# A hybrid layer pair: new order and new PSUM banks in the prepare stage of the recurrent branch

## The reference, cut to what matters

```python
us = token_shift(u_shift, mu[0], mu[1])             # r, k, v, w_in, a_in
w_log = -softplus(-(w0 + einsum('blde,def->dblf', tanh(w_in), w2))) - 0.5
decay = exp(-exp(w_log))                            # low-rank product 1, two directions d
a = sigmoid(a0 + einsum('blde,def->dblf', a_in, a2))   # low-rank product 2, the "rate"
kkf = to_heads(k * k_k)
kk = kkf * rsqrt(maximum(sum(kkf * kkf, -1), 1e-24))   # the norms
k_dir = to_heads(k)[None] * (1 + (a - 1) * to_heads(k_a)); b_dir = kk[None] * a
y = y_f + y_b                                       # of the two scans
yn = (y - mean) * rsqrt(var + LNX_EPS) * lnx_g + lnx_b
bonus = sum(r * (k_dir[0] + k_dir[1]) * r_k, -1) * v
out = (yn + bonus) * silu(gate)
```

## Time and profile before

| | |
|---|---|
| median of three runs | 3101.37 us |
| span of the profiled execution (first to last instruction) | 3091.2 us, 10.2 us below that median; the page gives no other time of that execution |
| busy: PE, DVE, ACT, POOL | 2874.3, 1512.4, 964.4, 771.8 us |
| the four prepare stages | 40.10, 44.70, 45.85 and 40.05 us, 170.70 us together |

### The profile page before, as it was taken

How to read it: one execution, slowest core, us unless ns; L and a number is a source line. 1 busy time by engine, 2 the same in 40 slices (tenths; PEclk the granted TensorE clock), 3 DMA queues, 4 the chain that set the end, 5 groups by cost and what they waited for, 6 DMA issues and landing times. The chain is left out here.

```text
span 3091.2 us, 61066 instructions
## 1 busy us (share of the span) xinstructions
PE 2874.3 (93%) x25648; PEld 2134.9 (69%) x25648; DVE 1512.4 (49%) x2768; ACT 964.4 (31%) x2248; POOL 771.8 (25%) x977
## 2 busy tenths in 40 slices
PE   6989998999998998999999989998999798999999
PEld 4968787886563786764588856645888576458674
DVE  5654636454433854541464246427833774265552
ACT  2021213122432124551221137511212574112561
POOL 3312223130013430011222214225531432244000
PEclk8999999999999999999999989999999899999999
DMA  6230100001332112121211152020111311212100
GB/s 225 81 113 19 39 4 16 17 32 59 110 103 101 55 55 96 56 83 41 83 52 47 66 188 77 11 95 34 55 55 55 124 55 56 87 47 89 58 1 28
DMA packets 108049, 206.16 MB, mean 67 GB/s; under 512 B 21795, under 2 KB 25394, under 8 KB 107264
## 3 DMA queue, kind: packets, MB, share of 16 engines
q1 hardware_dynamic: 107504, 201.36, 18.6%
q0 software_dynamic: 272, 0.89, 0.1%
HBM read 186.91 MB, written 15.54 MB: 65 GB/s over the span
## 5 line engine op out<-in xcount | busy, mean ns | idle before, releaser
L665 PE MATMUL psum<-weights,h_t 128*128 128x256 f32 x1488 | 352.0, 379 | 0.8 <-ACT p_u_u L749 0.8
L665 PEld LDWEIGHTS psum<-weights,h_t 128*128 128x128 f32 x1488 | 279.6, 190 | 38.5 <-ACT p_u_u L749 1.2
L1299 DVE TENSOR_REDUCE neg_max<-psum 128x1 f32<-128x768 f32 (+1 forms) x192 | 159.8, 864 | 220.4 <-PE psum L1169 174.8
L665 PE MATMUL psum<-z_l,x_tiles 128*128 128x256 f32 x816 | 192.8, 379 | 0.0
L665 PEld LDWEIGHTS psum<-z_l,x_tiles 128*128 128x128 f32 x816 | 155.0, 190 | 21.1
L1862 PE MATMUL psum<-weights,q_l 128*128 128x512 f32 x384 | 166.5, 592 | 0.0
L760 ACT ACTIVATE square<-psum 128x512 f32<-128x512 f32 (+1 forms) x80 | 45.0, 565 | 378.5 <-DVE psum L1017 242.0
L1190 PE MATMUL psum<-eye,prob 128*128 128x128 f32 x832 | 135.9, 286 | 11.3 <-DVE prob_t L1317 3.9
L1346 POOL TENSOR_TENSOR z_l<-z_l,inv_total 128x128 f32<-128x128 f32 x80 | 31.9, 399 | 428.7 <-DVE inv_total L1310 428.7
L1264 ACT ACTIVATE prob<-psum,neg_max 128x768 f32<-128x768 f32 (+1 forms) x160 | 129.7, 816 | 18.6 <-DVE neg_max L1299 12.4
L1862 PEld LDWEIGHTS psum<-weights,q_l 128*128 128x128 f32 x384 | 72.2, 190 | 87.1 <-issue 87.1
(11 more groups left out here) (445 smaller groups left out, 6175.9 us busy)
## 6 DMA issues: line engine op xcount, KB each, us to landing
weights<-in_ada_w_dram SPq DMA_DIRECT2D x30, 2048.0 KB, 8.0
weights<-in_a_w_in_dram SPq DMA_DIRECT2D x10, 2048.0 KB, 8.7
weights<-in_b_w_in_dram SPq DMA_DIRECT2D x8, 2048.0 KB, 9.2
weights<-in_c_w_in_dram SPq DMA_DIRECT2D x8, 2048.0 KB, 9.1
weights<-in_w_in_dram SPq DMA_DIRECT2D x6, 2048.0 KB, 7.7
x_aside<-x_tiles SPq DMA_DIRECT2D x24, 512.0 KB, 2.6
x_tiles<-x_aside SPq DMA_DIRECT2D x4, 3072.0 KB, 12.8
weights<-in_a_w_out_dram SPq DMA_DIRECT2D x4, 2048.0 KB, 8.0
```

What stands on the lines that cost most here:

```text
L665: last = pe.matmul(dst, lhs[:, k, :], rhs[k // 2][:, k % 2, :], start=k == 0, stop=k == KH - 1)
L1299: last = dve.tensor_reduce(neg_max[:, i % 4, m:m + 1], score(i, m, 0, keys), AX, ALU.max, negate=True)
```

## The change

All in the prepare stage; no instruction's operands change but for the banks:

- **PE.** The low-rank product of the decay comes first, before the norm sums, with both 256-column context parts (they now share bank 5); the 512-column part of the rate follows the norm sums. For p > 0 three eighths of the first projection stand before the spreading of the norms, the rest behind it. The low-rank products of d = 1 follow. y is turned before the last projection, v and the bonus rows after it. Pair 0 has one half of the modulation sums before the spreading, the other behind.
- **DVE.** The decay scan of d = 0 starts before kk is made; the last three operations on y come after direction 0, and y's gate after direction 1. DVE, in place of ACT, copies v and the bonus out of PSUM, at the end of the stage.
- **ACT** takes the first latent tile before the second `decays`, the second before the second `exponentials` (p > 0), and moves tile x - 1 between the square and the scaling of tile x.
- **POOL** raises the norms to their power before y's. The second `decays` waits for k_f only, not for r_f.

```diff
     def lat_bank(x):
-        return pr.bank(0 if x % 2 else 2)
+        return pr.bank(1 if x % 2 else 7)
 
     def turn_bank(x):
-        return pr.bank(3 if x % 2 else 1)
+        return pr.bank(3 if x % 2 else 2)
...
+                    move(x - 1)
                 if x >= 2:
                     act.wait_ge(*turned.at(x - 1))
...
                     act.activation(gate_rows[:, c, :], pr.bank(c), ACT.Copy).then_inc(*mod_copied.tick())
-            act.wait_ge(*v_turned.at(1))
-            if p:
-                act.wait_ge(*y_ready.at(1))
-            act.activation(b["v_tok"][:, 0:XC, :], pr.bank(1).rearrange("p (c i) -> p c i", i=HEAD), ACT.Copy)
-            act.activation(b["v_tok"][:, XC:NC, :], pr.bank(3)[:, 0:CTX].rearrange("p (c i) -> p c i", i=HEAD),
-                           ACT.Copy).then_inc(*bonus_out.tick())
-            early = 1 if units[0][0] == "kv" else 0
-            if early:
+            else:
                 take(0)
             decays(1)
-            if not early:
-                take(0)
+            take(1 if p else 0)
             exponentials(1)
-            for x in range(1, len(units)):
+            for x in range(2 if p else 1, len(units)):
...
             pool.wait_ge(*pool_chained.at(1))
+            pool.wait_ge(*norms.at(2))
...
-                    pe.matmul(pr.bank(5 + 2 * j)[:, 0:CTX], lora[s, j, P * p:P * p + P], src[s, GAP:US],
-                              start=True, stop=True).then_inc(*lora_done.tick())
+                src = (w_in, a_in)[j]
+                return pe.matmul(lora_ps(j)[ctx], lora[s, j, P * p:P * p + P], src[s, GAP:US] if ctx else src[s, 0:SEQ],
+                                 start=True, stop=True)
+
+            def lora_decay(d):
+
+                if d:
+                    pe.wait_ge(*exp_done.at(2))
+                lora_part(d, 0, 0)
+                lora_part(d, 0, 1)
+                lora_part(d, 1, 1).then_inc(*lora_done.tick())
+
+            def lora_rate(d):
+                lora_part(d, 1, 0).then_inc(*lora_done.tick())
...
                     pe.wait_ge(*moved.at(x - 1))
                 else:
-                    pe.wait_ge(*bonus_out.at(1))
+                    pe.wait_ge(*kk_done.at(1))
...
-                    w = pr.weights.get(pe, first_chunk + chunk_at[kind])
-                if x >= 2:
-                    pe.wait_ge(*read_out(x - 2))
-                elif x == 0:
-                    pe.wait_ge(*kk_done.at(1))
-                elif p:
-                    pe.wait_ge(*y_gated.at(1))
-                else:
-                    pe.wait_ge(*mod_copied.at(1))
...
+                    if x >= 2:
+                        pe.wait_ge(*read_out(x - 2))
+                    elif x and p == 0:
+                        pe.wait_ge(*mod_copied.at(2))
+                for f in range(a, e):
...
+            def turn_v():
+                pe.wait_ge(*exp_done.at(4))
...
+            def bonus_rows():
+                pe.wait_ge(*prods.at(1))
...
+            lora_decay(0)
+            norm_sums()
+            lora_rate(0)
             if p == 0:
-                pe.wait_ge(*mod_copied.at(2))
-            for c in range(NC):
-                for h in range(2):
-                    s = slice(64 * h, 64 * h + 64)
-                    last = pe.matmul(pr.bank(1 if c < XC else 3)[s, CH * (c % XC):CH * (c % XC) + CH],
-                                     v[s, col_of(c):col_of(c) + CH], pr.eye[s, s], start=True, stop=True)
-            last.then_inc(*v_turned.tick())
-            for x in range(len(units)):
+                mod_sums_of(0)
+                spread_norms()
+                mod_sums_of(1)
+            else:
+                project(0, 0, 3)
+                spread_norms()
+                project(0, 3, KT)
+            lora_decay(1)
+            lora_rate(1)
+            for x in range(1 if p else 0, len(units)):
                 project(x)
                 if x and x - 1 in lat:
                     turn(x - 1)
+                if p and x == len(units) - 2:
+                    turn_y()
             if p == 0:
-                pe.wait_ge(*exp_done.at(4))
                 for c in range(2):
                     mod_columns(pe, gate_sums[:, 8 * c:8 * c + 8], gate_rows[:, c, :], pick).then_inc(*mod_turned.tick())
...
+            turn_v()
+            bonus_rows()
             if len(units) - 1 in lat:
                 turn(len(units) - 1)
...
             y, bonus, square = b["y"][:, 0, :, :], b["bonus"][:, :, :], b["y_square"].rearrange("p (c i) -> p c i", c=XC)
+            for gap in (kk, dec, rate):
+                dve.memset(gap[:, SEQ:GAP], 0.0)
...
             if p:
+                link(dve.reduce_sum(stat[:, 1, :], square, AX))
+                dve.tensor_scalar(stat[:, 1, :], stat[:, 1, :], 1.0 / HEAD, LNX_EPS, ALU.mult, ALU.add)\
+                    .then_inc(*y_squared.tick())
                 link(dve.tensor_tensor(bonus, bonus, b["v_tok"][:, 0:XC, :], ALU.mult))
                 link(dve.tensor_tensor(bonus, bonus, wide(lnx[:, 1, previous, :], 1, XC), ALU.add))
-                dve.wait_ge(*y_rooted.at(1))
-                link(dve.tensor_tensor(y, y, wide(stat[:, 3, :], 2, HEAD), ALU.mult))
-                link(dve.tensor_tensor(y, y, wide(lnx[:, 0, previous, :], 1, XC), ALU.mult))
-                dve.tensor_tensor(y, y, bonus, ALU.add).then_inc(*y_ready.tick())
-            dve.wait_ge(*spread.at(1))
-            for gap in (kk, dec, rate):
-                dve.memset(gap[:, SEQ:GAP], 0.0)
-            dve.scalar_tensor_tensor(kk[:, 0:SEQ], k[:, 0:SEQ], kk_w, pr.bank(2), ALU.mult, ALU.mult)
-            dve.scalar_tensor_tensor(kk[:, GAP:US], k[:, GAP:US], kk_w, pr.bank(3)[:, 0:CTX], ALU.mult, ALU.mult)\
-                .then_inc(*kk_done.tick())
-            dve.wait_ge(*kk_done.at(1))
...
                 link(dve.tensor_tensor_scan(run[:, flip], resets[:, d, flip], dec[:, flip], 0.0,
                                             ALU.mult, ALU.add))
                 dve.tensor_tensor(ex[:, :], run[:, :], dec[:, :], ALU.subtract).then_inc(*summed.tick())
+                if d == 0:
+                    dve.wait_ge(*spread.at(1))
+                    dve.scalar_tensor_tensor(kk[:, 0:SEQ], k[:, 0:SEQ], kk_w, pr.bank(2), ALU.mult, ALU.mult)
+                    dve.scalar_tensor_tensor(kk[:, GAP:US], k[:, GAP:US], kk_w, pr.bank(3)[:, 0:CTX], ALU.mult, ALU.mult)\
+                        .then_inc(*kk_done.tick())
+                    dve.wait_ge(*kk_done.at(1))
                 dve.wait_ge(*exp_done.at(2 * d + 2))
...
                 dve.tensor_tensor(b["b_f"][:, d, :], rate[:, :], dec[:, :], ALU.mult)
-                link(dve.tensor_tensor(b["k_f"][:, d, :], kd[:, :], dec[:, :], ALU.mult))
+                dve.tensor_tensor(b["k_f"][:, d, :], kd[:, :], dec[:, :], ALU.mult).then_inc(*used.tick())
+                dve.wait_ge(*used.at(d + 1))
                 dve.wait_ge(*exps.at(d + 1))
-                dve.tensor_tensor(b["r_f"][:, d, :], b["r_f"][:, d, :], r, ALU.mult).then_inc(*used.tick())
+                dve.tensor_tensor(b["r_f"][:, d, :], b["r_f"][:, d, :], r, ALU.mult)
                 if d == 0 and p:
-                    dve.wait_ge(*y_turned.at(1))
-                    dve.tensor_tensor(mix_t[:, previous, :], pr.bank(0), gate_s[:, previous, :], ALU.mult)\
-                        .then_inc(*y_gated.tick())
+                    dve.wait_ge(*y_rooted.at(1))
+                    link(dve.tensor_tensor(y, y, wide(stat[:, 3, :], 2, HEAD), ALU.mult))
+                    link(dve.tensor_tensor(y, y, wide(lnx[:, 0, previous, :], 1, XC), ALU.mult))
+                    dve.tensor_tensor(y, y, bonus, ALU.add).then_inc(*y_ready.tick())
             dve.scalar_tensor_tensor(ksum[:, :], ksum[:, :], rk_w, r, ALU.mult, ALU.mult).then_inc(*prods.tick())
-            if p == 0:
+            if p:
+                dve.wait_ge(*y_turned.at(1))
+                dve.tensor_tensor(mix_t[:, previous, :], y_ps, gate_s[:, previous, :], ALU.mult)
+                dve.wait_ge(*y_ready.at(1))
+            else:
                 g = PCOL["ada_b"] + 16
                 dve.wait_ge(*mod_turned.at(2))
                 dve.tensor_tensor(pr.modulation[:, 16:24, :], gate_sums.rearrange("p (f v) -> p f v", v=2),
                                   wide(pr.par[:, g:g + 8], 2, 2), ALU.add)
+            dve.wait_ge(*v_turned.at(1))
+            dve.tensor_copy(b["v_tok"][:, 0:XC, :], v_x_ps.rearrange("p (c i) -> p c i", i=HEAD))
+            dve.tensor_copy(b["v_tok"][:, XC:NC, :], v_c_ps.rearrange("p (c i) -> p c i", i=HEAD))
```

More of the change, by code:

```diff
@@ L2575, in take @@
                     .then_inc(*lat_squared.tick())
+                if x and x - 1 in lat:
+                    move(x - 1)
                 if x >= 2:
@@ new lines, in spread_norms, with mod_sums_of @@
+            def spread_norms():
+                pe.wait_ge(*rooted.at(1))
+                for t in range(NT):
+                    for h in range(2):
```

(11 more changed lines are left out.)

114 lines of the change are left out of this document (50 added, 64 removed).

## The result

| | median us | runs, us | against before, 95% interval |
|---|---|---|---|
| before, the runs beside it | 3099.25 | 3096.72 to 3104.19 (4) | |
| changed kernel | 3069.22 | 3064.17 to 3074.45 (4) | 0.9914 [0.9896, 0.9932] |
| changed kernel again (experiment 1) | 3073.9 | 3071.26 to 3078.09 (6) | 0.9926 [0.9915, 0.9938] |

The change makes the kernel faster, by 30.0 us in the first set of runs and by 21.4 in the second, 0.7 to 0.9%. As a ratio to the median that I had (3101.37) the forecast was 0.9928, inside both intervals.

What follows compares the result with a forecast made beforehand. Bounds: the chain to kk, PE's mid-stage waits and leftover projections; in pair 0, a weights DMA. Stage gains 1.2 + 7.8 + 7.5 + 5.9 = 22.4 us made the span 3068.8, plus 10.2 around it 3079; range 3074 to 3085, with a clock fall 3073 to 3092.

Steps and rivals of the forecast that it cites:

- The base: Whole kernel: 10.2 us added around the forecast span of 3068.8 us, giving 3079 us.
- the sum of 22.4: Four prepare stages: shorter by 1.2, 7.8, 7.5 and 5.9 us in pairs 0, 1, 2 and 3.
- The runs' spread: Forecast's own range, 3074 to 3085 us: 3 us allowed for the spread of runs, 2 for semaphore delays.
- The clock in pairs 1 to 3: Starts of these stages: full clock, no fall, as 512-column products come first; before, 10.2 us low.
- rival A: Pairs 1 to 3: clock still falls for 10.2 us; gains only 10.8 us, 3090.6 us in all; chance 0.13.
- DVE's chain: Pairs 1 to 3: decay starts at 6.1 us, ahead of kk, against 12.7; ksum ready at 31.4, against 36.7.
- Pair 2's new wait: PE waits some 2 us for ACT's scaled row, ready at 28.1 us, before the third kv tile's transposes.
- The tail: End of pairs 1 and 2: y, v and bonus cover PE's old wait for ACT and POOL before the last transposes.
- Pair 3: Stage bound by DVE, ending in its copy of the bonus: 34.1 us against 40.05, 5.9 less.
- Pair 0's 1.2 us: Weights' chunk sent and first projection started 3.0 us sooner, less v's 1.6 and a copy's 0.1: net 1.2 less.
- B: Pairs 1 to 3: low clock lasts longer, making the kernel slower; 3111 us at 24 us per stage; chance 0.03.
- C: Stages shrink but what follows waits on its own clock, such as a weight chunk: 3098 to 3104 us; chance 0.04.

Runs made afterwards that it cites:

- 6: Changed kernel with the norm sums ahead of the low-rank products again, as before the change; ratio 0.9964 against before.
- 8: Kernel before with POOL's order alone changed, the norms' power first and y's variance second; ratio 1.0003 against before.
- 3: Changed kernel with v turned in pair 0's wait for the weights, into two other PSUM banks; 3073.11 us, ratio 0.9925 against before.
- 5: Changed kernel with kk computed ahead of the decay and scan of direction 0 again, as before the change; ratio 0.9958 against before.
- 9: Changed kernel with the last tile's transposes ahead of v and the bonus rows; ratio 0.9952 against before.
- 12: Changed kernel with v turned in pair 0's wait for the weights, run once more with more repeats; ratio 0.9927 against before.
- 4: Changed kernel with two unused 128-row by 256-column products behind the decay products in pairs 1 to 3; 3077.22 us, ratio 0.9938 against before.
- 7: Changed kernel with the whole first projection behind direction 1's low-rank products, none ahead of the spreading, in pairs 1 to 3; ratio 0.9963 against before.
- 2: Changed kernel with three projection steps ahead of the norm sums and two ahead of the spreading, pairs 1 to 3; 3081.0 us, ratio 0.9945 against before.
- 10: Changed kernel with projection steps ahead of norm sums and spreading, and y's variance and two bonus operations before DVE's maximum; 3074.72 us, ratio 0.9926 against before.
- 11: Changed kernel with v turned in pair 0's wait, projection steps in front and four DVE operations ahead of the maximum; 3074.84 us, ratio 0.994 against before.

## Why the prediction was wrong

**The base, which is the step that failed.** "With the 10.2 us around it that is 3079.0, and the median of the runs shown, 3101.4, lies 10.2 above the profiled span as well; so 3079." These are one number, used as its own check: the 10.2 us was median less span, and it was taken for a fixed cost around any span. That cost is 1.8 us; the other 8.4 was the distance between one execution (3093.0) and the median of three (3101.37). That median was high itself: the runs of before beside the experiments have medians of 3095.33, 3097.63, 3097.72 and 3097.53. From 3097.5 the sum of 22.4 gives 3075, and the range moves to 3069.1 to 3088.1, which just holds the 3069.22.

**The runs' spread.** The base is 3.9 us of the 9.8 by which the forecast was too high. Most of the rest is that the first four runs of the changed kernel lay low, as six later ones had a median of 3073.9. The share for the spread, 3 us, was too small for this: in the largest set, of 17, before ran from 3088.81 at a mean clock of 0.973 to 3104.59 at 0.968. A range on an absolute time has to hold this, however good the sum is.

**The gain** came out at 0.9928, measured 0.9926 and 0.9914, and part of that is luck. The stages were to give 22.4 us and gave 17.25 and 20.2 in the two profiles, in which the clock fell. The rest of the medians' 21.4 and 30.0 us isn't located: the profile of before is of an execution 4.5 us faster than the usual median, and no run shows where a usual one is longer. The span that was forecast, 3068.8, with the 1.8 us would have been 3070.6, close to the result only because two errors work against each other: a fast execution as the base, and stages summed without the fall.

**The clock in pairs 1 to 3**: wrong that there would be no fall, right that the new order shortens it. The clock in all 14 profiles, at the starts of these three stages:

| PE's order at the start | profiles | low at the start, us |
|---|---|---|
| norm sums first | before, 6, 8 | 10.2 in seven stages of nine, 13.7 and 6.8 in one each |
| as changed | first profile, 1, 3, 5, 9, 12 | 6.8 in twelve stages of 18, 3.4 in three, none in three |
| as changed, two idle products | 4 | 3.4 in all three |
| no projection ahead of the spreading | 7 | 10.2, 17.1, 6.8 |
| projection steps in front | 2, 10, 11 | none in all nine (3.4 in the middle of pair 2 in two profiles) |

So the fall goes with PE's order, and beside that it differs from one execution to the next. The prediction's own sign for rival A, a clock of about 0.5 near the start, did appear. It was A's event, shorter and cheaper: A had 3.6 us in pair 3 for 10.2 us of it, and 6.8 us cost 1.66. The Trainium skill's page TensorE: Matmul & The Clock Gate (What's actually happening) has sustained activity release the clock; here PE was busy for 6.80 of 6.80 us at half clock, three times, so the trace speaks again against that half of the rule, if activity means a busy PE. In pair 1 the clock came back at 336.90, when PE was in the projection's steps on 128 rows; the busy time before 333.47 was low-rank products and norm sums, on 64.

**Stages.**

| | before | forecast | after | with the clock nearest to the forecast's |
|---|---|---|---|---|
| pair 0 | 40.10 | 38.9 | 40.13 | 38.62 (no second fall, 9) |
| pair 1 | 44.70 | 36.9 | 39.38 | 36.07 (no fall, but kk first, 5) |
| pair 2 | 45.85 | 38.3 | 38.99 | not seen in this order |
| pair 3 | 40.05 | 34.1 | 34.95 | 33.29 (no fall, 1) |

Where the clock was as assumed, the hand sums were 0.3 to 0.8 us too long; with the clock as it fell, those of pairs 1 to 3 were 0.7 to 2.5 too short. *DVE's chain* was right: decay at 6.4 for 6.1, and the scan ahead of kk is worth 3.3 us in pairs 2 and 3 each (5). *Pair 2's new wait* was named rightly; its size was 1.15 instead of about 2:

```profile
486.34 0.47 ACT L2589 ACTIVATE rwkv_work<-psum,root 128x256 f32<-128x256 f32 x1 [1.11 <-POOL root L2634]
486.87 0.44 PE L2688 MATMUL psum<-eye,rwkv_work 128*128 128x128 f32 x2 [1.15 <-ACT rwkv_work L2589]
```

The row is scaled at 29.3 us, 1.2 later than I had; PE comes to it later still, since its own start ran at half clock. *The tail* of pairs 1 and 2 is worth 2 us each (9). *Pair 3* ends in DVE's copy of the bonus, ksum at 32.5 (31.4 forecast; 30.9 in experiment 1, where the clock didn't fall):

```profile
618.89 0.75 DVE L2835 SCALAR_TENSOR_TENSOR rwkv_work<-rwkv_work,params,shifted_late 128x512 f32<-128x512 f32 x1
619.91 1.10 PE L2734 MATMUL psum<-ones,rwkv_work 64*64 64x64 f32 x32
621.13 0.68 DVE L2849 COPY kept<-psum 128x512 f32<-128x512 f32 x1
```

*Pair 0's 1.2 us* were offset by its second fall: it followed the wait that v used to fill, which no term had. Without that fall the stage took 38.62 (9).

**The other rivals.** B fell: in pairs 1 to 3 the stages with longer falls (6, 7) were still shorter than before. C fell: span less the four stages was 2920.5 us before and 2916.4 to 2927.1 in the 12 profiled executions with the new order, where the stages' sum went from 147.2 to 164.4. The 4 us by which the changed kernel's first profile lies under before there are within this scatter.

**Open.** Why the clock stays up in some executions of one kernel and not in others; and why the totals of experiments 10 to 12 show none of what the stages gain. Part is falls behind the stage, but 364.37:456.55 above, at a clock of 1.00, is 1.5 to 1.8 us longer than the same stretch in the changed kernel's two profiles (367.10:457.47 and 365.32:456.02), and no experiment separates that. Nor is any of these parts tested alone: y's operations moved on DVE, v and the bonus copied by DVE instead of ACT, and ACT's order of the latent tiles. What experiments 5, 6, 7 and 9 cost doesn't add up to the gain, since the clock has a share in each.

## What to carry to other kernels

Add what lies around a span from runs that list both, never as median minus profiled span, and put the spread of the runs of before into the range whole. Before you move wide products to the front of a stage that starts on thin TensorE work, see what the vector chain behind the thin ones loses: here the fall at the start was gone in nine stages of nine, and the totals were no better. Some small work in an engine's wait is worth keeping there: pair 0's stage was 2.7 us shorter with it, though the 2.7 us were not seen in the total.
